# Experts sorted by count and paired by it, with three column tiles a pair and the last pair's output added on chip

## The reference, cut to what matters

```python
g_sel = argmax(softmax(t @ w_grp))                  # one group of 4
top_v, top_i = top_k(softmax(le_g), 2)              # two experts of its 8
combine = g_w * one_hot(g_sel) * within             # (320, 32), two non-zeros a row
hid = einsum('nd,edf->nef', t, w_ein)               # 1024 -> 512 for each expert
a, b = split(hid, 2)
act = silu(a) * b * combine
out = einsum('nef,efd->nd', act, w_eout)            # 256 -> 1024
x = x + g2 * out;  y = rms_norm(x, norm_final_g)
```

## Time and profile before

| | us |
|---|---|
| time, median of 3 runs | 906.89 (905.81 to 906.90) |
| profiled execution, its own time | 910.62 |
| its span in the trace | 908.8 |
| PE busy | 748.5 (82%) |
| DVE / ACT / POOL busy | 264.8 / 163.4 / 81.5 |
| DMA moved | 238.57 MB, mean 263 GB/s |

### The profile page before, as it was taken

How to read it: one execution, slowest core, us unless ns; L and a number is a source line. 1 busy time by engine, 2 the same in 40 slices (tenths; PEclk the granted TensorE clock), 3 DMA queues, 4 the chain that set the end, 5 groups by cost and what they waited for, 6 DMA issues and landing times.

```text
span 908.8 us, 10592 instructions
## 1 busy us (share of the span) xinstructions
PE 748.5 (82%) x3868; PEld 404.8 (45%) x3868; DVE 264.8 (29%) x796; ACT 163.4 (18%) x401; POOL 81.5 (9%) x119
## 2 busy tenths in 40 slices
PE   2999999999999876877789995469978869688634
PEld 2636666555666552434357674333322323222212
DVE  0224323012000696655513214731110111101026
ACT  2012443111000562222210011101110101101002
POOL 0000000023000243000000000110110010110100
PEclk9999999999999899787979997659998999999766
DMA  9958667452450392799989704217999999998151
GB/s 360 399 199 314 237 247 286 173 229 93 160 211 0 135 375 99 256 393 350 353 359 424 316 0 185 58 33 301 425 423 424 421 424 422 425 420 334 61 118 58
DMA packets 51369, 238.57 MB, mean 263 GB/s; under 512 B 8930, under 2 KB 17122, under 8 KB 39090
## 3 DMA queue, kind: packets, MB, share of 16 engines
q1 hardware_dynamic: 42834, 223.93, 62.9%
q0 software_dynamic: 6176, 11.83, 3.8%
q10 hardware_dynamic: 2304, 2.10, 0.7%
HBM read 236.43 MB, written 18.09 MB: 280 GB/s over the span
## 4 chain that ended last, share of the span: by engine, by line
PE 67%; DMA 18%; DVE 9%; issue 3%; ACT 1%; SPq 1%; POOL 0%; POOLq 0%; DVEq 0%; ACTq 0%
PE bank L484 15%; DMA arena<-in_w_ein 15%; PE bank L845 8%; PE bank L457 6%; PE bank L778 4%; PE bank L787 4%; PE bank L865 4%; PE bank L440 2%; PE bank L527 2%; PE bank L738 2%; PE bank L681 2%; PE bank L492 2%; DMA arena<-in_w 1%; PE bank L704 1%; DMA arena<-y_rows 1%
## 5 line engine op out<-in xcount | busy, mean ns | idle before, releaser
L845 PE MATMUL bank<-arena 128*64 128x512 f32 x544 | 138.0, 666 | 33.3 <-DMA arena<-in_w_ein 31.4
L484 PE MATMUL bank<-arena 128*128 128x320 f32 x512 | 141.7, 433 | 0.0
L484 PEld LDWEIGHTS bank<-arena 128*128 128x128 f32 x512 | 95.7, 189 | 45.3 <-issue 6.4
L845 PEld LDWEIGHTS bank<-arena 128*64 128x64 f32 x544 | 42.1, 152 | 118.2 <-issue 84.4
L865 PE MATMUL bank<-arena 128*64 128x512 f32 x272 | 62.1, 598 | 1.4 <-issue 1.4
L1635 DVE COPY arena<-bank 128x512 f32<-128x512 f32 x17 | 11.8, 691 | 162.3 <-PE bank L834 162.3
L457 PE MATMUL bank<-arena 128*128 128x512 f32 x128 | 56.8, 594 | 0.0
L1099 ACT ACTIVATE arena<-bank 128x256 f32<-128x256 f32 x17 | 6.5, 385 | 180.1 <-PE bank L845 180.1
L1761 POOL DMA_INDIRECT y_rows<-arena,rows_of_slots_out x17 | 17.1, 1004 | 231.7 <-DVE arena L1649 231.7
L787 PE MATMUL bank<-arena 128*128 128x320 f32 x128 | 34.8, 432 | 1.5 <-DVE arena L1487 1.5
L457 PEld LDWEIGHTS bank<-arena 128*128 128x128 f32 x128 | 23.4, 187 | 28.5 <-issue 28.3
(11 more groups left out here) (313 smaller groups left out, 889.7 us busy)
## 6 DMA issues: line engine op xcount, KB each, us to landing
arena<-in_w_ein SPq DMA_DIRECT2D x16, 4096.0 KB, 34.2
arena<-in_w_eout SPq DMA_DIRECT2D x16, 2048.0 KB, 24.8
arena<-in_w_ada SPq DMA_DIRECT2D x12, 2048.0 KB, 8.8
arena<-in_w_in SPq DMA_DIRECT2D x10, 2048.0 KB, 10.0
arena<-in_k_pages SPq DMA_DIRECT2D x64, 320.0 KB, 6.5
arena<-in_v_pages SPq DMA_DIRECT2D x64, 320.0 KB, 10.0
arena<-in_cmp_pages SPq DMA_DIRECT2D x48, 128.0 KB, 9.3
arena<-in_win SPq DMA_DIRECT2D x16, 256.0 KB, 5.3
```

What stands on the lines that cost most here:

```text
L484: m = mm(banks[c % 4][:, 0:N], ring[q][:, k, P * (c % 4):P * (c % 4 + 1)], hT[:, k, :], start=(k == 0), stop=(k == KD - 1))
L845: m = mm(banks[2 + p % 2][CAP * e:CAP * (e + 1), :], xeT[p % 2][:, k, CAP * e:CAP * (e + 1)], wi2[p % 3][:, e, k, :], start=(k == 0), stop ...
```

## The change

Experts 0 to 5 stay where they are (pairs 0 to 2, 64 slots each, loaded before routing is known). The other 26 are ranked by their number of rows. The 13 with most rows get 96 slots, the 13 with fewest get 32; rank r of the first half is paired with rank 25-r of the second, in a tile of 128 slots, from pair 3 on. Where 64-slot tiles are not used, PE computes with three column tiles: 0:64 and 64:96 with the first expert's weights, 96:128 with the second's. Extra tiles are made only for what is over 96, 64 or 32. SP reads the expert numbers from a table that DVE writes, and loads each expert with a DMA of its own; for pair 15 `w_ein` comes in two halves.

Pair 15 is not scattered. Its output stays in `yeS[0]`; PE does its three steps after the output of pair 14. `y_rows` is zeroed near the start, since rows of pair 15 are no longer written there. PE brings the reloaded rows into the banks by products with the identity, as an accumulation that stays open, and closes it with a product of pair 15's output and a one-hot table `last_hit` of slots by rows, 320 columns wide. Banks 6 and 7 still hold pair 15's output, so their chunks come after it is evacuated. DVE writes the table of extra tiles after its first copy of rows instead of before it.

```diff
 CAP = 64
 EXTRA = 10
 PAIRS = E // 2
+FIXED = 6
+FREE_E = E - FIXED
+HEAVY = 96
+LAST = PAIRS - 1
...
+        def y_slot(p):
+
+            return p % 3 if p < PAIRS else 1 + (p - PAIRS) % 2
+
+        def y_used(p):
+
+            return 16 * (p // 3) if p < PAIRS else 16 * (LAST // 3 + (p - PAIRS) // 2)
...
+            sp.wait_ge(s_ord, 1)
             for p in range(3, PAIRS):
+                of = [sp.value_load(order[0:1, r:r + 1], min_val=0, max_val=E - 1) for r in (p - 3, FREE_E + 2 - p)]
                 sp.wait_ge(s_hd, p - 2)
-                pair_in(p)
+                if p < LAST:
+                    for u in range(2):
+                        sp.dma_start(wi2[p % 3][:, u].rearrange("p k n -> p (k n)"),
+                                     w_ein[bass.ds(of[u], 1), :, :].rearrange("o p n -> (o p) n")).then_inc(s_wi[p % 3], 16)
+                else:
+                    for part, s in ((0, s_wi[p % 3]), (1, s_wil)):
+                        for u in range(2):
+                            sp.dma_start(wi2[p % 3][:, u, 4 * part:4 * part + 4].rearrange("p k n -> p (k n)"),
+                                         w_ein[bass.ds(of[u], 1), :, 2048 * part:2048 * part + 2048].rearrange("o p n -> (o p) n"))\
+                                .then_inc(s, 16)
                 sp.wait_ge(s_od, 2 * (p - 2))
-                pair_out(p)
+                for u in range(2):
+                    sp.dma_start(wo2[p % 3][:, u].rearrange("p k n -> p (k n)"),
+                                 w_eout[bass.ds(of[u], 1), :, :].rearrange("o p n -> (o p) n")).then_inc(s_wo2[p % 3], 16)
...
+            def tiles_of(p):
+
+                if 3 <= p < PAIRS:
+                    return [(0, 64, 0), (64, 32, 0), (HEAVY, 32, 1)]
+                return [(0, CAP, 0), (CAP, CAP, 1)]
+
...
-                    for e in range(2):
-                        m = mm(banks[2 + p % 2][CAP * e:CAP * (e + 1), :], xeT[p % 2][:, k, CAP * e:CAP * (e + 1)],
-                               wi2[p % 3][:, e, k, :], start=(k == 0), stop=(k == KD - 1))
+                    if p == LAST and k == 4:
+                        te.wait_ge(s_wil, 32)
+                    for r, n, e in tiles_of(p):
+                        m = mm(banks[2 + p % 2][r:r + n, :], xeT[p % 2][:, k, r:r + n], wi2[p % 3][:, e, k, :],
+                               start=(k == 0), stop=(k == KD - 1))
...
-                        for e in range(2):
-                            m = mm(banks[6 + half][CAP * e:CAP * (e + 1), :], actT[:, p % 2, j, CAP * e:CAP * (e + 1)],
+                        for r, n, e in tiles_of(p):
+                            m = mm(banks[6 + half][r:r + n, :], actT[:, p % 2, j, r:r + n],
                                    wo2[p % 3][:, e, j, 512 * half:512 * (half + 1)], start=(j == 0), stop=(j == 1))
...
-            for p in range(PAIRS):
+            for p in range(LAST):
                 hidden(p)
-                if p + 1 < PAIRS:
-                    turn_rows(p + 1)
+                turn_rows(p + 1)
                 if p:
                     pair_output(p - 1)
                 turn_act(p)
-            pair_output(PAIRS - 1)
+            pair_output(LAST - 1)
+            hidden(LAST)
+            turn_act(LAST)
+            pair_output(LAST)
...
-            for t in range(4):
-                te.wait_ge(s_ysum, t + 1)
-                for c in range(KD):
-                    m = te.transpose(banks[c][:, RT * t:RT * (t + 1)], yR[0:RT, t, 0, P * c:P * (c + 1)], ident[0:RT, 0:RT])
-                    if t == 3:
-                        m.then_inc(s_yt, 1)
+            for chunks in (range(6), range(6, KD)):
+                if chunks[0]:
+                    te.wait_ge(s_yA, PAIRS)
+                    te.wait_ge(s_yD, PAIRS)
+                for t in range(4):
+                    te.wait_ge(s_ysum, t + 1)
+                    for c in chunks:
+                        mm(banks[c][:, RT * t:RT * (t + 1)], yR[0:RT, t, 0, P * c:P * (c + 1)], ident[0:RT, 0:RT],
+                           start=(t == 0), stop=False)
+            for c in range(KD):
+                mm(banks[c][:, 0:N], yeS[y_slot(LAST)][:, P * c:P * (c + 1)], last_hit, start=False, stop=True).then_inc(s_yt, 1)
...
+                if p == LAST:
+                    sc.wait_ge(s_od, p * 2 + 2)
+                    act(yeS[y_slot(p)][:, 512:1024], banks[7][:, :], ACT.Copy, scale=wtab[:, p:p + 1]).then_inc(s_yD, 1)
...
+            link(ve.scalar_tensor_tensor(key[R], cnt[R], float(E), cst[R, C_E:C_E + E], ALU.mult, ALU.subtract))
+            link(ve.tensor_tensor(beaten, key[R, FIXED:E].unsqueeze(1).to_broadcast(every),
+                                  key[R, FIXED:E].unsqueeze(2).to_broadcast(every), ALU.is_gt))
+            link(ve.tensor_reduce(rank[R], beaten, AX, ALU.add))
+            ve.tensor_scalar(less[R], rank[R], FREE_E / 2 - 0.5, None, ALU.is_ge)
+            ve.tensor_scalar(up[R], rank[R], float(P), 3.0 * P, ALU.mult, ALU.add)
+            link(ve.tensor_scalar(put[:, FIXED:], rank[R], -float(P), (FREE_E + 2.0) * P, ALU.mult, ALU.add))
+            ve.tensor_tensor(up[R], up[R], put[:, FIXED:], ALU.min)
+            link(ve.tensor_scalar(room[:, FIXED:], less[R], 32.0 - HEAVY, float(HEAVY), ALU.mult, ALU.add))
+            ve.tensor_copy(pos[R], banks[1][R, 0:4 * E].rearrange("p (t e) -> p t e", e=E))
+            link(ve.scalar_tensor_tensor(put[:, FIXED:], less[R], float(HEAVY), up[R], ALU.mult, ALU.add))
+            wholei = whole_i[:, :]
+            link(ve.tensor_tensor(more[R], cnt[R], room, ALU.subtract))
+            link(ve.tensor_scalar(wholei, more[R], 0.0, CAP - 1.0, ALU.max, ALU.add))
+            link(ve.tensor_scalar(wholei, wholei, 6, None, ALU.logical_shift_right))
+            link(ve.tensor_copy(more[R], wholei))
...
+            same = cst[0:1, C_TRI:C_TRI + FREE_E * FREE_E].rearrange("p (r e) -> p r e", e=FREE_E)
+            wide1 = [1, FREE_E, FREE_E]
+            link(ve.tensor_tensor(same, cst[0:1, C_E:C_E + FREE_E].unsqueeze(2).to_broadcast(wide1),
+                                  rank[0:1].unsqueeze(1).to_broadcast(wide1), ALU.is_equal))
+            link(ve.tensor_tensor(same, same, cst[0:1, C_E + FIXED:C_E + E].unsqueeze(1).to_broadcast(wide1), ALU.mult))
+            link(ve.tensor_reduce(key[0:1, 0:FREE_E], same, AX, ALU.add))
+            ve.tensor_copy(order[:, :], key[0:1, 0:FREE_E]).then_inc(s_ord, 1)
...
+            at_last = at(rt + 1752, 3)
+            for k in range(3):
+                m = ve.tensor_scalar(at_last[:, k:k + 1], none[:, LAST:PAIRS], -float(P) * k, None, ALU.add)
+            link(m)
+            for k, (t0, tn) in enumerate(TOK):
+                ve.tensor_scalar(last_hit[:, t0:t0 + tn], cst[:, C_ROW:C_ROW + tn], at_last[:, k:k + 1], None, ALU.is_equal)
...
+            po.dma_start(y_rows.rearrange("(t p) d -> p t d", p=P),
+                         zeros.unsqueeze(1).to_broadcast([P, 2 * N // P, D])).then_inc(s_zf, 16)
...
+                if p == LAST:
+                    po.memset(xeS[p % 3], 0.0).then_inc(s_z, 1)
+                    po.wait_ge(s_z, 7)
...
-            for p in range(PAIRS):
+            for p in range(LAST):
...
-                    po.wait_ge(s_ys[p % 3], 16 * (p // 3 + 1))
+                    po.wait_ge(s_ys[y_slot(p)], y_used(p) + 16)
             for k in range(3):
-                po.wait_ge(s_ys[k], 16 * ((PAIRS - 1 - k) // 3 + 1))
-            po.memset(wtab, 0.0).then_inc(s_ya, 1)
+                po.wait_ge(s_ys[k], 16 * LAST // 3)
+            po.memset(cst[:, C_SIN:C_SIN + 1], 0.0).then_inc(s_ya, 1)
```

More of the change, by code:

```diff
@@ L64 @@
 C_E = C_LT + 128
-C_HALF = C_E + E
+C_PUT = C_E + E
+C_ROOM = C_PUT + E
+C_HALF = C_ROOM + E
 C_ROW = C_HALF + 2
@@ L1570, in _ @@
             ends = [at(rt + 1400 + 48 * k, 48) for k in range(2)]
-            link(ve.tensor_copy(pos[R], banks[1][R, 0:4 * E].rearrange("p (t e) -> p t e", e=E)))
+            put, room = cst[R, C_PUT:C_PUT + E], cst[R, C_ROOM:C_ROOM + E]
+            key, rank, less, up = at(rt + 1624, E), at(rt + 1656, FREE_E), at(rt + 1688, FREE_E), at(rt + 1720, FREE_E)
+            every = [RT, FREE_E, FREE_E]
+            beaten = cst[R, C_TRI:C_TRI + FREE_E * FREE_E].rearrange("p (e f) -> p e f", f=FREE_E)
             link(ve.tensor_copy(cnt[R], banks[1][R, 4 * E:5 * E]))
-            link(ve.tensor_scalar(more[R], cnt[R], CAP + 0.5, None, ALU.is_ge))
-            for n in range(2, N // CAP):
-                link(ve.scalar_tensor_tensor(more[R], cnt[R], n * CAP + 0.5, more[R], ALU.is_ge, ALU.add))
+            link(ve.scalar_tensor_tensor(key[R], cnt[R], float(E), cst[R, C_E:C_E + E], ALU.mult, ALU.subtract))
[14 more added lines that the diff above has]
+            link(ve.tensor_copy(more[R], wholei))
             for k in range(2):
@@ L1585, in _ @@
             link(ve.tensor_tensor(far[R], end, more[R], ALU.subtract))
-            link(ve.tensor_scalar(far[R], far[R], float(CAP), float(CAP * (E - 1)), ALU.mult, ALU.add))
```

(38 more changed lines are left out.)

45 lines of the change are left out of this document (22 added, 23 removed).

## The result

The changed kernel takes 1012.48 us (median of 4 runs, 1007.65 to 1019.98) against 906.89 (905.81 to 910.18) before: the ratio is 1.114, 95% interval 1.109 to 1.120. 1002 was forecast, within 975 to 1035. The profiled execution spans 1005.8 us; the sum gave 1004.7.

The account below looks back on a forecast made before the run. The expert loop was taken as DMA-bound, becoming PE-bound: 643.4 to start pair 3, 20.9 for it, 278.3 for pairs 4 to 14, last products to 976.4, then 9.5 and 18.75: span 1004.7, forecast 1002 us, range 975 to 1035.

Parts of the forecast that it names:

- the sum: Whole kernel: stage times added from hidden(3) at 643.4 to a span of 1004.7 us in the profiled execution's time.
- 2.8 us of slack a pair: Expert loop before: PE needs 12.0 us a pair, the weights' DMA 14.8, so 2.8 can hide added PE work.
- the 31.4 us of waits: Expert loop before: PE's 10 waits for `in_w_ein`, forecast to go once PE is the bound.
- The price of a step: Expert loop from pair 3: unequal tiles take turns, 1.99 us a step instead of 0.88; hidden 15.9 us, output 8.0.
- The argument that disjoint columns wait too: Expert loop: inference that unequal tiles wait even on disjoint columns, from gaps of 0.54 and 0.52 us after the last record.
- The rival with all three side by side (873): Expert loop: step stays 0.88 us, loop stays DMA-bound, 873 us (-34); chance 0.12.
- The other rivals: Expert loop: three rounds a step (899 us, chance 0.04); turns at halved clock (near 1330, 0.02); extra pass stays (excluded).
- The routing: Before the expert loop: added DVE operations to lay out the slots cost 3.1 us (2 to 5).
- The end: Last output to first residual: 9.5 us instead of 45.4, from 1.5 for count and branches, 7.4 identity records, 0.6 one-hot.
- My upper bound of 0.166 a record: Tail's 64 identity records: spacing taken as 0.115 us, at most 0.166, from today's eight in 1.33 us at lower clock.
- "Cover" of the reload: End of loop: evacuation, scatter, reload and last sum, 21.1 us, hide beside pair 15's 25.8 us on PE.
- From span to median: Whole kernel: profiled execution 1.8 us longer than its span and 3.7 over the median, so 1004.7 becomes 1002.8, said as 1002.

Follow-up runs that it names:

- the run with two tiles that don't touch: Changed kernel without the middle tile (slots 64 to 95 of pairs 3 to 15 not computed), leaving columns 0:64 and 96:128: 1001.67 us, ratio 1.103 to before.

## Why the prediction was right

**The bound and its change.** Right in every step: DMA-bound with 2.8 us of slack a pair, PE-bound after, the 31.4 us of waits gone. Eleven turns of 25.2 us can be counted off in the chain.

**The price of a step.** 1.99 us from L681 and L686 gave 15.9 and 8.0; 15.88 and 7.94 were measured. The argument that disjoint columns wait too, the weakest link, rested on 0.02 us in two rows; the run with two tiles that don't touch settled it. The rival with all three side by side (873) was what the machine does for equal widths (887.71), so its chance of 0.12 was a chance on this one rule. The other rivals are out: no third round was saved, and the clock stayed at 1.00.

**The routing.** 3.1 us forecast. The two large operations took 0.86 and 0.85 as interpolated. Counted from DVE's first operation on the counts (L1571 at 580.93 before, L1624 at 575.95 after) to the first gathered rows on PE (601.30 and 598.51), the stretch is 20.4 and 22.6 us: 2.2 more.

**The start.** Not foreseen, and no effect of an edit that I could show: the loop began 2.8 us earlier than before the change instead of 3.1 later, since the attention part ended 5.6 us sooner in this execution (5.0 are left where the routing's arithmetic begins, and the routing takes 2.2 of them). Other kernels with the same code there spread over 12 us.

**The end.** The failed term: 9.5 us from last output to first residual, measured 16.6. The step as put was "reading the extra count and five branches not taken, about 1.5 us" and 64 records at 0.115. Measured: 2.9 us each for two of the five branches; the first lay under the output, the second left PE idle for 2.85 us. Then the granted clock fell to its 1.2 GHz level behind the first 14 of the 64 records (0.64 on average from 970 to 987), so they took 12.5 us instead of 7.4; the prediction had carried them at full clock. My upper bound of 0.166 a record came from single-record transposes and was too low for two-record products at that clock (0.213). These 7 us were hidden in the sum by the 5.9 of the start: that the span came within 1.1 us of the sum is luck, what was understood is the loop. "Cover" of the reload was right: the sums were done at 968.4, before the last output ended at 970.4.

**From span to median.** I took the median 3.7 us under the profiled execution, as before. It came 4.8 over it (1012.48 against 1007.65). That is most of the 10 us by which 1002 missed.

## What to carry to other kernels

Column tiles of one width ran side by side here, tiles of 64 and 32 columns took turns even on columns that don't touch: pad to one width, even with more products, before mixing the two. A second thing to check is what stands between the last heavy product and the tail: skipped code had a price in the branch, and the small records behind it ran in part at the lower clock. Work that is moved off a wait gains only if the unit that takes it over is still running at full speed.

## What the runs showed of the hardware that was not expected

Of five conditional branches in a row on PE's sequencer, each over one unrolled pass that is not run, one or two took 2.7 to 3.2 us without other traffic and one took 7.6 to 7.7 us in the two kernels where it fell beside the reload of 2.6 MB; the others took 0.2 to 0.4. With a single such branch it took 0.23, beside the reload too. Each long one spans the arrival of one 16 KB packet on the `instruction` queue, which started 5.0 us into the branch beside the reload and 0.3 to 0.4 us into it elsewhere.

The records of 80x80 are spaced 0.11 us at the full granted clock and 0.213 at the lower. The lower one came during or behind 2 to 7 us of idle PE in some kernels, and in the run with two tiles that don't touch among the same records with no idle before them.
